# Second attention: scores from rounded high parts and remainders instead of one float32 product

## The reference, cut to what matters

```
qx = apply_rope_2(rms_norm_2(split_heads(aq, N_Q_HEADS, HEAD_DIM), q_norm), cos, sin)
kx = apply_rope_2(rms_norm_2(split_heads(ak, N_KV_HEADS, HEAD_DIM), k_norm), cos, sin)
kc = rms_norm_2(split_heads(ak_c, N_KV_HEADS, HEAD_DIM), k_norm)
attn_x = gqa_attention(qx, concatenate([kx, kc]), concatenate([vx, vc]))

def gqa_attention(q, k, v):        # per block of 128 queries
    s = einsum('bqhgd,bkhd->bhgqk', q_blk, k) * (HEAD_DIM ** -0.5)
    p = softmax(s)
    return einsum('bhgqk,bkhd->bqhd', p, v)
```

## Time and profile before

| | us |
|---|---|
| three runs of the kernel | 1834.95, 1837.07, 1830.63 |
| their median | 1834.95 |
| span of the profiled execution, first to last instruction | 1833.2 |
| PE busy in the span | 1752.1 (96%) |
| DVE, ACT, POOL busy | 1007.4, 798.5, 718.5 |

### The profile page before, as it was taken

How to read it: one execution, slowest core, us unless ns; L and a number is a source line. 1 busy time by engine, 2 the same in 40 slices (tenths; PEclk the granted TensorE clock), 3 DMA queues, 4 the chain that set the end, 5 groups by cost and what they waited for, 6 DMA issues and landing times.

```text
span 1833.2 us, 24795 instructions
## 1 busy us (share of the span) xinstructions
PE 1752.1 (96%) x8879; PEld 1401.9 (76%) x8879; DVE 1007.4 (55%) x1553; ACT 798.5 (44%) x1359; POOL 718.5 (39%) x795
## 2 busy tenths in 40 slices
PE   7999999988999889999999999999999999999998
PEld 5777787766777557777878888888878778888887
DVE  6688786677547773456659738656633342212122
ACT  4345463556456663345542244554432342323131
POOL 3645544443443105321114432123234645555563
PEclk9999999999999999999999999999999999999999
DMA  6342422221322001210028611111123323333332
GB/s 200 94 125 81 138 70 84 67 70 46 82 79 68 24 12 51 67 47 24 24 96 270 209 47 40 41 48 49 45 80 96 100 70 102 94 97 98 93 97 98
DMA packets 238797, 152.09 MB, mean 83 GB/s; under 512 B 7997, under 2 KB 223046, under 8 KB 238694
## 3 DMA queue, kind: packets, MB, share of 16 engines
q1 hardware_dynamic: 225758, 125.50, 24.1%
q10 hardware_dynamic: 12936, 25.21, 4.1%
HBM read 148.59 MB, written 2.10 MB: 82 GB/s over the span
## 4 chain that ended last, share of the span: by engine, by line
PE 73%; issue 8%; DVE 7%; ACT 6%; POOL 5%; DMA 1%; POOLq 0%; ACTq 0%; DVEq 0%; SPq 0%
PE ps L650 19%; PE ps L654 18%; PE ps L651 18%; POOL wl L600 5%; PE ps L2130 2%; PE ps L2112 1%; PE ps L1589 1%; PE ps L1621 1%; PE ps L2597 1%; PE ps L2119 1%; ACT wh L613 1%; PE ps L2563 1%; PE ps L2113 1%; DVE queries L1875 1%; PE ps L2567 1%
## 5 line engine op out<-in xcount | busy, mean ns | idle before, releaser
L600 POOL TENSOR_TENSOR wl<-raw,wh 128x256 fp32r<-128x256 f32 (+1 forms) x775 | 695.0, 927 | 1056.5 <-ACT wh L613 1056.5
L650 PE MATMUL ps<-ah,wh 128*128 128x512 f32 (+1 forms) x1144 | 466.2, 408 | 15.9 <-DVE al L762 9.1
L654 PE MATMUL ps<-ah,wl 128*128 128x512 f32 (+1 forms) x1144 | 451.1, 394 | 0.3
L651 PE MATMUL ps<-al,wh 128*128 128x512 f32 (+1 forms) x1144 | 450.5, 394 | 0.0
L613 ACT ACTIVATE wh<-raw 128x1024 fp32r<-128x1024 f32 (+1 forms) x220 | 230.8, 1049 | 319.1 <-PE ps L654 307.9
L650 PEld LDWEIGHTS ps<-ah,wh 128*128 128x128 f32 (+1 forms) x1144 | 216.5, 189 | 73.2 <-issue 19.8
L654 PEld LDWEIGHTS ps<-ah,wl 128*128 128x128 f32 (+1 forms) x1144 | 216.1, 189 | 51.2 <-POOL wl L600 2.1
L651 PEld LDWEIGHTS ps<-al,wh 128*128 128x128 f32 (+1 forms) x1144 | 216.4, 189 | 45.3 <-issue 1.7
L650 PE MATMUL ps<-bh,wh 128*128 128x512 f32 (+1 forms) x588 | 234.7, 399 | 9.4 <-DVE resid L1449 3.7
L654 PE MATMUL ps<-bh,wl 128*128 128x512 f32 (+1 forms) x588 | 231.3, 393 | 0.4 <-POOL wl L600 0.4
L651 PE MATMUL ps<-bl,wh 128*128 128x512 f32 (+1 forms) x588 | 231.1, 393 | 0.0
(11 more groups left out here) (426 smaller groups left out, 2695.4 us busy)
## 6 DMA issues: line engine op xcount, KB each, us to landing
raw<-w_mlp SPq DMA_DIRECT2D x64, 512.0 KB, 4.0
raw<-w_in SPq DMA_DIRECT2D x52, 512.0 KB, 3.8
raw<-ssm_w_in SPq DMA_DIRECT2D x40, 512.0 KB, 3.8
ada_late<-w_ada ACTq DMA_DIRECT2D x16, 1024.0 KB, 6.6
ada_raw<-w_ada ACTq DMA_DIRECT2D x16, 512.0 KB, 4.0
raw<-ssm_w_out SPq DMA_DIRECT2D x16, 512.0 KB, 3.4
raw<-mla_w_in SPq DMA_DIRECT2D x11, 512.0 KB, 3.9
raw<-mla_w_out SPq DMA_DIRECT2D x8, 512.0 KB, 3.9
```

The lines of the kernel that those rows point to most:

```text
L600: nc.gpsimd.tensor_tensor(wl[:, s, part], raw[:, s, part], wh[:, s, part].bitcast(F32), ALU.subtract).then_inc(lo_ready, LOW_PIECES * (par ...
L650: nc.tensor.matmul(dst, w_hi[k], x_hi[k], start=k == 0, stop=False)
L651: nc.tensor.matmul(dst, w_hi[k], x_lo[k], start=False, stop=False)
L654: ins = nc.tensor.matmul(dst, w_lo[k], x_hi[k], start=False, stop=k == n - 1)
```

## The change

Queries and keys are kept in two parts. DVE now scales the queries in place in `p_cos`. ACT copies them into a rounded `q_hi` (`high_q`), and DVE subtracts to get the remainder `q_lo` (`low_q`). The keys stay in `k_feat`; ACT makes `k_hi` (`high_k`, 768 columns), DVE `k_lo` (`low_k`). A score is the sum of `q_hi·k_hi`, `q_hi·k_lo` and `q_lo·k_hi`, for 512 and for 256 keys. The turned keys of head 1 pass through `k_feat` instead of `q_feat`. Where DVE and PE waited for `q_ready` and `k_ready` they wait for `q_low` and `k_low`. Besides, the semaphores by which chunk sums of squares are counted for three norms become two shared ones; no instruction but their counts changes there.

```
-            ins.then_inc(sem(name + "_squared"), 1)
+            ins.then_inc(sem("chunk_squared"), 1)
...
-        q_feat = r("q_feat", [P, 2, T])
+        q_hi, q_lo = r("q_hi", [P, 2, T], F32R), at("q_lo", [P, 2, T], F32R, gos_at)
+        k_hi, k_lo = (at(f"k_{n}", [P, KVH, TA], F32R, ARENA_END + k * KVH * TA * 4) for k, n in enumerate(("hi", "lo")))
...
-        k_cos = (p_cos[:], q_feat[:, 1])
+        k_cos = (p_cos[:], k_feat[:, 1, 0:T])
...
                 if n < 2:
-                    pe.wait_ge(sem("k_ready"), n + 1)
+                    pe.wait_ge(sem("k_low"), n + 1)
                 if t == 0:
-                    pe.wait_ge(sem("q_ready"), j + 1)
+                    pe.wait_ge(sem("q_low"), j + 1)
                 if n >= 2:
                     pe.wait_ge(sem("g_exp"), n - 1)
-                q = q_feat[:, j % 2, t * P:(t + 1) * P]
-                nc.tensor.matmul(bank(b), q, k_feat[:, j // QPK, 0:T], start=True, stop=True)
-                nc.tensor.matmul(bank(b + 1)[:, 0:CTX], q, k_feat[:, j // QPK, T:TA], start=True, stop=True).then_inc(sem("g_scores"), 1)
+                tile = slice(t * P, (t + 1) * P)
+                terms = ((q_hi, k_hi), (q_hi, k_lo), (q_lo, k_hi))
+                for cols, dst in ((slice(0, T), bank(b)), (slice(T, TA), bank(b + 1)[:, 0:CTX])):
+                    for k, (q, keys_) in enumerate(terms):
+                        ins_ = nc.tensor.matmul(dst, q[:, j % 2, tile], keys_[:, j // QPK, cols], start=k == 0, stop=k == 2)
+                ins_.then_inc(sem("g_scores"), 1)
...
+            def high_k(n):
+                act.wait_ge(sem("k_ready"), n + 1)
+                nc.scalar.activation(k_hi[:, n], k_feat[:, n], ACT.Copy).then_inc(sem("k_high"), 1)
+
+            def high_q(j):
+                act.wait_ge(sem("q_ready"), j + 1)
+                if j >= 2:
+                    act.wait_ge(sem("g_scores"), TT * (j - 1))
+                nc.scalar.activation(q_hi[:, j % 2], p_cos[:], ACT.Copy).then_inc(sem("q_high"), 1)
...
             scale_k(0)
+            high_q(0)
+            high_k(0)
             scale_k(1)
+            high_k(1)
             exp(0)
...
                 if n + 1 < NQ:
                     exp(n + 1)
+                if t == 2 and j + 1 < QH:
+                    high_q(j + 1)
...
                 if n == 0:
-                    dve.wait_ge(sem("q_ready"), 1)
+                    dve.wait_ge(sem("q_low"), 1)
...
+            def low_k(n):
+                dve.wait_ge(sem("k_high"), n + 1)
+                nc.vector.tensor_tensor(k_lo[:, n], k_feat[:, n], k_hi[:, n].bitcast(F32), ALU.subtract).then_inc(sem("k_low"), 1)
+
+            def low_q(j):
+                dve.wait_ge(sem("q_high"), j + 1)
+                nc.vector.tensor_tensor(q_lo[:, j % 2], p_cos[:], q_hi[:, j % 2].bitcast(F32), ALU.subtract).then_inc(sem("q_low"), 1)
...
-                nc.vector.tensor_tensor(q_feat[:, j % 2], p_cos[:], p_rstd[:, 0:T], ALU.mult).then_inc(sem("q_ready"), 1)
+                nc.vector.tensor_tensor(p_cos[:], p_cos[:], p_rstd[:, 0:T], ALU.mult).then_inc(sem("q_ready"), 1)
...
             scale_q(0)
+            low_q(0)
             rotate_k(0)
             rotate_k(1)
             scale_k(0)
+            low_k(0)
             scale_k(1)
+            low_k(1)
             top(0)
...
                 if n + 1 < NQ:
                     scale(n + 1)
+                if t == 2 and j + 1 < QH:
+                    low_q(j + 1)
```

More of the change, by code:

```diff
@@ L687, in norm_pe_summed @@
             nc.tensor.matmul(bank(b), ones[:], src, start=True, stop=True).then_inc(norm_sq_used, 1)
+        SQUARED_AT = {"mla": 0, "final": DC, "norm2": 2 * DC}
+        SUMMED_AT = {"mla": 0, "final": DC + 1, "norm2": 2 * DC + 3}
         def square_chunk(act, name, src, s, gain=None):
@@ L694, in square_chunk @@
                 ins = nc.scalar.activation(norm_sq[:, s + 1], src, ACT.Square, scale=gain)
-            ins.then_inc(sem(name + "_squared"), 1)
+            ins.then_inc(sem("chunk_squared"), 1)
         def sums_clear(dve, name, kinds=1):
-            nc.vector.memset(norm_v[:, 1:1 + kinds], 0.0).then_inc(sem(name + "_summed"), 1)
+            nc.vector.memset(norm_v[:, 1:1 + kinds], 0.0).then_inc(sem("chunk_summed"), 1)
         def sum_chunk(dve, name, c, s, kinds=1):
-            dve.wait_ge(sem(name + "_summed"), c + 1)
-            dve.wait_ge(sem(name + "_squared"), c + 1)
+            dve.wait_ge(sem("chunk_summed"), c + (SUMMED_AT[name] + 1))
+            dve.wait_ge(sem("chunk_squared"), c + (SQUARED_AT[name] + 1))
             nc.vector.tensor_tensor(norm_v[:, 1:1 + kinds], norm_v[:, 1:1 + kinds], norm_sq[:, s:s + kinds],
-                                    ALU.add).then_inc(sem(name + "_summed"), 1)
+                                    ALU.add).then_inc(sem("chunk_summed"), 1)
         def sums_end(dve, name):
-            dve.wait_ge(sem(name + "_summed"), DC + 1)
+            dve.wait_ge(sem("chunk_summed"), SUMMED_AT[name] + DC + 1)
             dve.sem_inc(norm_sq_ready, 1)
@@ L1956, in dve_between @@
         def dve_between(dve):
-            dve.wait_ge(sem("final_summed"), DC + 1)
-            nc.vector.scalar_tensor_tensor(norm_v[:, 2], norm_v[:, 1], EPS, norm_v[:, 2], ALU.mult, ALU.add).then_inc(sem("final_summed"), 1)
-            dve.wait_ge(sem("final_summed"), DC + 2)
+            dve.wait_ge(sem("chunk_summed"), SUMMED_AT["final"] + DC + 1)
+            nc.vector.scalar_tensor_tensor(norm_v[:, 2], norm_v[:, 1], EPS, norm_v[:, 2], ALU.mult, ALU.add).then_inc(sem("chunk_summed"), 1)
+            dve.wait_ge(sem("chunk_summed"), SUMMED_AT["final"] + DC + 2)
             dve.sem_inc(norm_sq_ready, 2)
@@ L2286, in turn_q @@
                 if j:
-                    dve.wait_ge(sem("q_ready"), j)
-                    dve.wait_ge(sem("k_ready"), KVH)
+                    dve.wait_ge(sem("q_low"), j)
+                    dve.wait_ge(sem("k_low"), KVH)
                 st.wait()
@@ L2297, in scale_q @@
                 st.wait()
-                if j >= 2:
-                    dve.wait_ge(sem("g_scores"), TT * (j - 1))
-                nc.vector.tensor_tensor(q_feat[:, j % 2], p_cos[:], p_rstd[:, 0:T], ALU.mult).then_inc(sem("q_ready"), 1)
+                nc.vector.tensor_tensor(p_cos[:], p_cos[:], p_rstd[:, 0:T], ALU.mult).then_inc(sem("q_ready"), 1)
             def take_v(part):
```

## The result

| | before | after |
|---|---|---|
| median of the runs, us | 1836.01 (4 runs, 1830.63 to 1837.93) | 1849.65 (4 runs, 1847.63 to 1850.01) |
| span of the profiled execution, us | 1833.2 | 1848.0 |

A forecast was written before the change was run, and what follows sets the result against it. PE was taken as the bound, with thin margins for `q_feat` and `k_feat`. Entry 8.0, six heads 4.1, last head 2.0 and tail −0.5 made +13.6 us on 1833.2, plus 1.75 to the median: 1848.5, range 1843 to 1854.

The forecast's parts named there:

- PE's products: Score blocks on PE: six rounded products take 1.05 us instead of 1.29, giving back 0.24 in each of 32 blocks.
- Rival 4: Score products of 256 columns are paced by weight loads, 0.19 us each instead of 0.12; 1852.9 us; chance 0.04.
- The entry chain: Score loop entry: `high_q(0)` through `low_k(0)` delays `scores(0)` by 7.3 us with PE idle, and `top(0)` by 8.0.
- From there to `sum_q(1)`: Entry, from `top(0)` on: waits run over DVE and ACT, shorter scores don't help, `sum_q(1)` comes 8.0 us later, once.
- at about 809 … 1.8 us are free; if the clock is back by 812, nothing is lost: Behind `scores(1)`: PE has 4.8 us of work before `sum_q(1)`, leaving 1.8 us of slack against half clock.
- rival 1: Entry's 7 us PE gap lowers TensorE's clock, `sum_q(1)` up to 3.0 us later; 1848.5 to 1851.5 us; chance 0.20.
- The heads: Six head changes: PE stalls 1.40 us, first piece +0.24, shorter blocks −0.96; +0.68 each, +4.1 us in all.
- The last head: Seventh head change, with no projection to cover the chain: scores start 2.0 us later; wait for `q_lo` of 2.8.
- The tail: Last four score blocks save 0.24 us each, half counted because the softmax chain ends there too: −0.5 us.
- A sign that missed: Entry: PE was to idle 2 to 2.5 us before `scores(1)`.
- Rivals 2: Entry and heads: everything added stays hidden beside PE, the 7.7 us won whole; 1827.3 us; chance 0.05.
- 3: Entry costs 8.0 us but the head change is covered, +1.3 in all; 1836.2 us; chance 0.07.

The follow-up runs named there:

- run 5: Changed kernel with 28 unused rounded matmuls of 512 columns in PE's queue ahead of `scores(0)`, filling the entry's gap; 1846.17 us, ratio 1.007.
- run 2: Changed kernel with query scaling, `high_q` and `low_q` at t = 2 moved ahead of the next block's softmax pieces; 1841.69 us, ratio 1.0046.
- run 6: Changed kernel with the edits of run 1 and run 2 together; 1835.81 us, ratio 1.0001.
- run 7: Run 6 with key head 1's scaling and splitting behind the first softmax pieces, `scores(1)` no longer waiting for them; 1835.51 us, ratio 1.0005.
- run 8: Run 7 with DVE ending the next head's query rotation at t = 1, before scaling the probabilities; 1828.84 us, ratio 0.9973.
- run 10: Run 8 with scores as one float32 product of `q_hi` and `k_hi`, remainders made but left out; 1837.61 us, ratio 1.0011.
- run 3: Changed kernel with scores as one float32 product of `q_hi` and `k_hi`, remainders made but left out; 1854.0 us, ratio 1.012.
- run 1: Changed kernel with the first `high_q` on ACT moved right behind `scale_q(0)`, ahead of `take_k(1)`; 1842.56 us, ratio 1.0049.

## Why the prediction was right

- **PE's products.** Forecast 1.05 for six rounded products, measured 1.04 (row 831.28). Rival 4 (0.19 for 256 columns) is out: three and three products would have taken 1.26.
- **The entry chain.** `scores(0)` was forecast 7.3 us later and came 7.3 later (805.41 against 797.96, less the 0.11 by which this execution runs late). Two errors in it cancel. I took 1.10 for `low_q(0)` beside POOL, by the row of 1.15; it took 0.69, though POOL ran from 794.03 to 797.37. Against it, the steps I left in the roundings aren't all 0.02: at three places of this chain 0.10 to 0.13 us stand between a piece and the one that depends on it (796.78 to 796.90, 802.28 to 802.41, 805.31 to 805.41). `top(0)` came 7.8 later (808.74 against 800.91), or 7.7 less the 0.11, forecast 8.0.
- **From there to `sum_q(1)`.** The step "at about 809 … 1.8 us are free; if the clock is back by 812, nothing is lost" decided, and it wasn't back: half clock until 814.8. Nor was the slack where I had counted it, in PE's work ahead of `sum_q(1)`, since PE still idled 0.34 us there; the lower clock came in through ACT's wait for the projection of the queries of head 1. The nine projection products from 810.96 on stand 0.43 us apart instead of 0.23, ACT gets their result at 815.03 only, and `sum_q(1)` comes 9.25 later, not 8.0. Run 5 and the waits of ACT tell the two apart: 7.7 for the chain, 1.57 for the clock. So rival 1 came true beside the forecast, in the middle of its price (0 to 3.0). The Trainium skill ("TensorE: Matmul & The Clock Gate", section on why this matters for your kernels) warns of such gaps between bursts, and the trace agrees: 0.50 behind 7.17 us of idle time.
- **The heads.** Stall forecast 1.40, measured 1.34; first block behind it +0.24, measured +0.28 (1.32 − 1.04); four shorter blocks −0.96, measured −1.0. Net +0.68, measured 3.54 / 6 = +0.59. ACT's `high_q` was hidden as forecast: it ended at 824.93, and DVE was free at 825.26.
- **The last head.** +2.0, measured +1.87: idle 2.46 in place of 0.57, where I had named 2.8.
- **The tail.** Here the sign was wrong: −0.5 forecast, +0.92 measured. I had asked what the gap at the entry does to the clock and not what the stall of the last head does. Behind it the clock is 0.50 from 948.0 to 951.4. In runs 2, 6 and 7, where that stall is 1.37, the clock holds, and the tail is 18.69 or 18.70 us instead of 19.86: −0.25 without the clock, which costs 1.2.
- **The sum.** The two shares of the clock, 1.57 and 1.2 us, are more than the 2 us by which the stretch exceeds the forecast; the chains, read without the clock, came out 0.8 us below it. That the differences of the medians still agree to 0.1 us is chance: they scatter by more around the stretch (table above).
- **A sign that missed.** PE waited 1.20 us before `scores(1)`, not 2 to 2.5: `scores(0)` ran at half clock and ended later. In run 5, where it ran at full clock, the wait is 2.17.
- **Rivals 2 and 3** (everything hidden; the heads covered) were wrong for this order of instructions, but not for this arithmetic: runs 8 and 10 hide all of it at the heads.

## What to carry to other kernels

A cheaper product on the bound engine is worth its saving only where that engine is never made to wait for the operands' new forms: count the chain that makes them, from its last event to the engine's wait, against the work the engine has in that time. Here 0.25 us a block were won and 1.34 us a head were lost by it, until the small pieces that PE waits for stood ahead of those that are needed later. Move the pieces first, then judge the arithmetic; the same operations made 1849.65 us in one order (1836.01 before) and 1827.21 in another (1833.45 before, in that set).

## What the runs showed of the hardware

- **The idle time right before it does not settle alone whether the clock falls, or for how long.** Behind 7.17 us of idle time it lay at its lower level for 13.7 us in the changed kernel and 10.2 in runs 2 and 3. Behind 2.46 or 2.45 us before the last head it fell in the changed kernel and runs 1 and 5, and behind 2.17 or 2.18 us before `scores(1)` in runs 1, 5 and 6, for 3.4 us each time; behind 2.45 us before the last head of run 3 it did not fall. In run 7 it held behind 2.97 us, in run 8, with the same work up to there (2.96), it fell for 3.4 us. Why is open; no run was made for it.
- **It stayed low while PE worked without a break**: from 809 to 813 us PE was busy for 4.00 of 4.00 us at 0.50.
- **DVE beside POOL.** A subtraction of two tiles in SBUF took 0.69 us while POOL's splitting ran (796.09), and the multiplication at 795.45 before took 1.15 beside the same work. The Trainium skill ("SBUF — State Buffer", section on the two separate sides) says that a VectorE operation with two SBUF inputs and a GpSimd operation that reads SBUF exclude each other on a shared pair of ports; the second row would fit that, the first doesn't show it. What tells them apart wasn't tried.
